# Output projection of a hybrid encoder block: high tokens against all four weight operands, then low tokens

## The chip, the cores and the metric

The kernel runs on one core of a Trainium2 chip. The metric is the device time of one execution in microseconds (us). The text speaks of the core's engines by their names in the profile: PE is TensorE's matmuls and PEld its weight loads, DVE is VectorE, ACT ScalarE, POOL GpSimd, SP the engine that issues most transfers.

## What is computed

One block over 2048 tokens and 16 meta tokens of width 1024, all in float32. Cut to what matters here:

```python
for layer in range(DEPTH):                                   # DEPTH = 1
    z = rms_norm(h, norm_gain[layer])
    proj = jnp.einsum("bld,de->ble", z, w_in[layer])
    q, k, v, g_attn, u_pool, g_pool = jnp.split(proj, SPLIT_POINTS, axis=-1)
    ...
    o_attn = chunked_window_attention(q, k, v, attn_sinks[layer])
    o_pool = multiscale_pool_mixer(u_pool, w_pool[layer], pool_scale[layer])
    gated = jnp.concatenate([jax.nn.silu(g_attn) * o_attn, jax.nn.silu(g_pool) * o_pool], axis=-1)
    h = h + jnp.einsum("ble,ed->bld", gated, w_out[layer])
return rms_norm(h, final_norm_gain)[:, N_META:]
```

The change is in the last product, `gated` (2048 tokens x 2048) times `w_out` (2048 x 1024).

## The kernel before, in words

**Splitting.** Every float32 operand of a large product is split into a high part (what the type fp32r keeps) and a low part (the rest). A product is then three matmuls: high times high, high times low and low times high. ScalarE makes the high part with a copy (L455 for weights, L651 for the tokens of the output projection), VectorE the low part with a subtraction (L694, L933).

**Stages.** The tokens are worked in two halves of 1024 (`h`). In each half come: the norm and the transposes of `x` (L1040); stage A, 18 blocks of input projection (function `project`, L1003 to L1005, weight blocks as stationary operand, 512 tokens as moving operand, all 24 matmuls of a call into one PSUM bank); stage B, 16 blocks of attention, each with scores (L1159 to L1161, four banks in turn), a projection block, transposes of the probabilities (L1185, L1187) and the product with the values (L1200 to L1203, one bank, `OB`); and stage C, the output projection (L1226 to L1228).

**Stage C.** It runs over two groups of 512 tokens (`tg`), and in each over 16 steps (`e`), one for each 128 rows of `w_out`: 64 steps in the whole kernel. A step holds four token tiles `t` of 128 tokens. For a tile the stationary operand is the tile's 128 x 128 block of gated tokens, high (`g_h`, from `gsh`) or low (`g_l`, from `gsl`), and the moving operand is 512 of the 1024 columns of the weight block, high (`w_h`) or low (`w_l`), for `dh` = 0 and 1. Tile `t` and column half `dh` have PSUM bank 2t + dh, so the eight banks hold the group's 512 x 1024 outputs and are summed over all 16 steps. A step is 24 matmuls. Weight blocks, their splits and the split tokens have two slots that alternate.

**What sets the order.** The instructions of each engine are written out by hand and held together by semaphores. For stage C:

- TensorE waits once at the head of a step for the low weights (`w_lo`) and the low tokens (`gs_lo`, or `gs_first` for the first step of a half). In the first step of a group it waits also ahead of some or all tiles, until the banks of that tile are free (`h_add`, `o_gate`, `pb_free`).
- The last matmul of a step signals `c_used`; ScalarE waits for it before it writes the high weights and high tokens of the step after next into the slot (L455, L651), VectorE follows (L694, L933), and SP may then load the next weight block into the raw slot (L264, waits for `w_lo`). GpSimd counts `c_used` too before it issues the loads of residual rows and of the next half's `x` (L428, L431).
- In the last step of a group the last matmul of each tile signals `c_done`. VectorE then adds the residual (L937), and the final norm and the store follow. In the very last group the last two steps are run for tiles 0 and 1, then 2, then 3.

The matmuls of a tile stand in the innermost loops of `step` (L1223 to L1228):

```python
for dh in range(2):
    w_h, w_l = wh[:, slot, dh * TB:dh * TB + TB], wl[:, slot, dh * TB:dh * TB + TB]
    co = ps[:, 2 * t + dh, :]
    te.matmul(co, g_h, w_h, start=first, stop=False)
    te.matmul(co, g_h, w_l, start=False, stop=False)
    last = te.matmul(co, g_l, w_h, start=False, stop=final)
```

Of the kernel before, what the change touches and what calls it, by code (L numbers as in the profile page):

```python
# [24 lines left out]
TB = 512  # L25
# [25 lines left out]
def build(nc, x, meta, wa, wu, wb, wp, wo, gain_n, gain_f, consts, ident_d, rot, rot_meta, out):  # L51
    wc = nc.dram_tensor("wc", (NG, 2, P, KT * P), F32, kind="Internal").ap()
    ctx = ExitStack()
    with ctx:
# [82 lines left out]
        wh, wl = wsplit[:, :, 0, :], wsplit[:, :, 1, :]  # L137
# [9 lines left out]
        ps = ctx.enter_context(nc.psum_tensor("ps", [P, 8, TB], F32))  # L147
# [55 lines left out]
        def block_c(h, tg, e):  # L203
            return BLOCKS * h + A_TILES + B_BLOCKS + C_STEPS * tg + e
# [769 lines left out]
        def _(pe):  # L974
            te = nc.tensor
# [93 lines left out]
            for h in range(HALVES):  # L1069
# [33 lines left out]
                if h == 0:  # L1103

                    pe.wait_ge(zm_step, 4)
                    for k in range(KT):
                        last = te.transpose(ps[:, SPARE, k * META:k * META + META], meta_rows[:, k * P:k * P + P], ident[0:META, 0:META])
# [22 lines left out]
                for m in range(NTT):  # L1130
                    last = te.transpose(ps[:, m // 4, (m % 4) * P:(m % 4) * P + P], wsum[:, m * P:m * P + P], ident[:, :])
# [17 lines left out]
                with pe.Fori(0, NG) as g:  # L1149
                    for sub in range(4):  # L1150
                        n = NCH * h + 4 * g + sub
                        slot = sub % 2

                        pe.wait_ge(qs_ready, n + 1)
                        for u in range(4):
# [5 lines left out]
                            last = te.matmul(so, q_l, k_h, start=False, stop=True)  # L1161
# [24 lines left out]
                        for u in range(4):  # L1186
                            last = te.transpose(ps[0:32, 2, u * P:u * P + P], probs[:, u, META0:KPITCH], ident[:, :])  # L1187
# [18 lines left out]
                for tg in range(TG):  # L1206
                    def step(e, slot, first=False, final=False, ts=range(TPG)):
                        pe.wait_ge(w_lo, block_c(h, tg, e) + 1)
                        if tg == 0 and first:
                            pe.wait_ge(gs_first, h + 1)  # L1210
                        else:
                            pe.wait_ge(gs_lo, (C_BLOCKS - 1) * h + C_STEPS * tg + e)
                        for t in ts:
                            if first and tg > 0:

                                pe.wait_ge(h_add, NTT * h + (tg - 1) * TPG + t + 1)
                            elif first and t == OB // 2:
                                pe.wait_ge(o_gate, NCH * (h + 1) + CREDIT)
                            elif first and t == PB[0] // 2:
                                for tb in range(NTB):  # L1220
                                    pe.wait_ge(pb_free[tb], FREES * (h + 1) + CREDIT)
                            g_h, g_l = gsh[:, slot, t * P:t * P + P], gsl[:, slot, t * P:t * P + P]
                            for dh in range(2):  # L1223
                                w_h, w_l = wh[:, slot, dh * TB:dh * TB + TB], wl[:, slot, dh * TB:dh * TB + TB]
                                co = ps[:, 2 * t + dh, :]
                                te.matmul(co, g_h, w_h, start=first, stop=False)  # L1226
                                te.matmul(co, g_h, w_l, start=False, stop=False)  # L1227
                                last = te.matmul(co, g_l, w_h, start=False, stop=final)  # L1228
                            if final:
                                last.then_inc(c_done, 1)  # L1230
                        if not final:
                            last.then_inc(c_used, 1)

                    step(0, 0, first=True)
                    step(1, 1)
                    with pe.Fori(1, C_STEPS // 2 - 1) as i:
                        step(2 * i, 0)
                        step(2 * i + 1, 1)
                    if h + 1 < HALVES or tg + 1 < TG:
                        step(C_STEPS - 2, 0)  # L1240
                        step(C_STEPS - 1, 1, final=True)
                    else:

                        for ts in ([0, 1], [2], [3]):
                            step(C_STEPS - 2, 0, ts=ts)
                            step(C_STEPS - 1, 1, final=True, ts=ts)
# [79 lines left out]
```

## Time and profile before

| | |
|---|---|
| median of 3 runs | 1353.28 us (1351.34 to 1355.07) |
| the profiled execution | 1353.39 us |
| its span, first to last instruction | 1351.7 us |
| mean granted TensorE clock | 0.994 |
| matmuls, and their busy time | 6293, 1318.0 us |
| of these in stage C | 1536 (L1226 to L1228) |

A busy time counts an engine's records with overlaps once. The records of consecutive matmuls overlap, since a matmul's record runs until its results are out and the next one has long started; so the distance from one start to the next is read from the timeline, not from the durations. Weight loads have records of their own (PEld) under the line of their matmul. An idle time with an arrow names what ended it.

### The profile page before, as it was taken

How to read it: one execution, taken by the hardware profiler on the slowest of the kernel's cores; microseconds unless marked ns; L12 is line 12 of the kernel's file. 1: busy time of each engine (PE TensorE's matmuls, PEld its weight loads, DVE VectorE, ACT ScalarE, POOL GpSimd, SP SyncE). 2: the span in 40 equal slices, each digit the busy share in tenths (PEclk: the TensorE clock that was granted, in tenths of full speed). 3: DMA queues.
4: the chain of work that ended last, by engine and by line, in shares of the span. 5: the costliest groups of instructions: out<-in, count | busy, mean ns of one | idle time of the engine just before them, and what ended most of it. 6: DMA issues, size and time to landing. Idle time of an engine off the chain costs nothing.

```text
span 1351.7 us, 18022 instructions
## 1 busy us (share of the span) xinstructions
PE 1318.0 (98%) x6293; PEld 1095.8 (81%) x6293; DVE 763.8 (57%) x1035; ACT 530.0 (39%) x1202; POOL 193.8 (14%) x260
## 2 busy tenths in 40 slices
PE   8899999999999999999999999999999999999997
PEld 8788888878787877888888888888878787788886
DVE  7443444476767675336456534447777767533635
ACT  6432222344444443225335222224444444322423
POOL 1121111211111111000001211121111111000000
PEclk8899999999999999999999999999999999999999
DMA  8511111110000004434442211110001010233442
GB/s 331 187 47 47 47 47 50 44 32 31 31 31 31 31 31 156 155 124 156 168 142 89 69 47 47 47 47 32 32 31 38 27 44 31 93 124 109 156 162 102
DMA packets 30397, 109.61 MB, mean 81 GB/s; under 512 B 3424, under 2 KB 3456, under 8 KB 30368
## 3 DMA queue, kind: packets, MB, share of 16 engines
q1 hardware_dynamic: 22032, 79.18, 17.0%
q0 software_dynamic: 8336, 30.05, 6.5%
q8 instruction: 17, 0.28, 0.1%
q14 instruction: 12, 0.10, 0.0%
HBM read 96.63 MB, written 12.58 MB: 81 GB/s over the span
## 4 chain that ended last, share of the span: by engine, by line
PE 58%; issue 28%; DVE 9%; DMA 2%; POOL 1%; ACT 1%; SPq 0%; DVEq 0%; POOLq 0%; ACTq 0%
PE ps L1227 9%; PE ps L1228 9%; PE ps L1226 9%; PE ps L1003 6%; PE ps L1004 6%; PE ps L1005 6%; DVE wsum L873 3%; PE ps L1185 2%; DVE stat L860 2%; DVE stat L863 1%; PE ps L1159 1%; PE ps L1161 1%; PE ps L1160 1%; PE ps L1187 1%; PE ps L1201 1%
## 5 line engine op out<-in xcount | busy, mean ns | idle before, releaser
L1003 PE MATMUL ps<-zh,wsplit 128*128 128x512 f32 x1072 | 422.4, 394 | 0.0
L1004 PE MATMUL ps<-zl,wsplit 128*128 128x512 f32 x1072 | 418.8, 391 | 0.0
L1005 PE MATMUL ps<-zh,wsplit 128*128 128x512 f32 x1072 | 418.1, 390 | 0.0
L694 DVE TENSOR_TENSOR wsplit<-wraw,wsplit 128x1024 fp32r<-128x1024 f32 x132 | 196.5, 1488 | 237.6 <-ACT wsplit L455 237.6
L1005 PEld LDWEIGHTS ps<-zh,wsplit 128*128 128x128 f32 x1072 | 201.4, 188 | 42.7
L1003 PEld LDWEIGHTS ps<-zh,wsplit 128*128 128x128 f32 x1072 | 201.5, 188 | 40.7 <-DVE wsplit L694 0.3
L1004 PEld LDWEIGHTS ps<-zl,wsplit 128*128 128x128 f32 x1072 | 201.5, 188 | 39.1
L455 ACT ACTIVATE wsplit<-wraw 128x1024 fp32r<-128x1024 f32 x132 | 139.7, 1058 | 227.2 <-PE ps L1228 217.3
L1228 PE MATMUL ps<-wsplit,gsl 128*128 128x512 f32 x512 | 203.3, 397 | 0.0
L1227 PE MATMUL ps<-wsplit,gsh 128*128 128x512 f32 x512 | 203.0, 396 | 0.0
L1226 PE MATMUL ps<-wsplit,gsh 128*128 128x512 f32 x512 | 199.7, 390 | 2.8 <-POOL gsl L413 2.5
L612 ACT ACTIVATE probs<-ps,stat 128x144 f32<-128x144 f32 x256 | 93.7, 388 | 133.8 <-DVE stat L863 133.8
L1226 PEld LDWEIGHTS ps<-wsplit,gsh 128*128 128x128 f32 x512 | 98.4, 192 | 26.3 <-issue 3.3
L1227 PEld LDWEIGHTS ps<-wsplit,gsh 128*128 128x128 f32 x512 | 96.2, 188 | 21.8
L1228 PEld LDWEIGHTS ps<-wsplit,gsl 128*128 128x128 f32 x512 | 96.2, 188 | 19.9
L355 POOL TENSOR_TENSOR rotsrc<-rotsrc,cos_t 128x1024 f32<-128x1024 f32 x18 | 61.6, 3420 | 324.5 <-DVE swapped L775 324.5
L595 ACT ACTIVATE wsum<-ps 128x512 f32<-128x512 f32 x64 | 38.5, 602 | 168.8 <-PE ps L1005 161.1
L795 DVE SCALAR_TENSOR_TENSOR gates_all<-wsum,ps 128x512 f32 x64 | 43.7, 682 | 73.3 <-ACT wsum L595 73.3
L396 POOL TENSOR_TENSOR kmask<-qk,cst 128x128 f32<-128x128 f32 x32 | 14.2, 443 | 385.6 <-PE ps L1161 385.1
L645 ACT ACTIVATE pth<-ps 128x512 fp32r<-128x512 f32 x64 | 34.8, 596 | 76.2 <-PE ps L1187 76.2
L539 ACT ACTIVATE rotsrc<-ps 128x512 f32<-128x512 f32 x32 | 19.1, 598 | 105.2 <-PE ps L1005 105.2
L775 DVE LOAD_MASK_SELECT swapped<-rotsrc x18 | 0.3, 14 | 104.8 <-issue 104.8
(160 smaller groups left out, 1575.2 us busy)
## 6 DMA issues: line engine op xcount, KB each, us to landing
wraw<-in_wo SPq DMA_DIRECT2D x64, 512.0 KB, 3.3
wraw<-in_wa SPq DMA_DIRECT2D x36, 512.0 KB, 3.3
wraw<-wc SPq DMA_DIRECT2D x16, 512.0 KB, 3.2
wraw<-in_wb SPq DMA_DIRECT2D x16, 512.0 KB, 3.2
rows<-in_x POOLq DMA_DIRECT2D x16, 512.0 KB, 4.3
xr<-in_x POOLq DMA_DIRECT2D x12, 512.0 KB, 5.6
curaw<-in_wu SPq DMA_DIRECT2D x8, 512.0 KB, 8.1
wc<-cout POOLq DMA_DIRECT2D x8, 512.0 KB, 4.5
```

Source lines behind the costliest of these rows:

```text
L355: gp.tensor_tensor(rotsrc[:, :], rotsrc[:, :], cos_t[:, :], ALU.mult).then_inc(rot_cos, 1)
L455: sc.activation(wh[:, slot, 0:size], wraw[:, slot, 0:size], ACT.Copy).then_inc(w_hi, 1)
L612: i = sc.activation(probs[:, u, kv * KEYS:kv * KEYS + KEYS], ps[:, u, kv * KEYS:kv * KEYS + KEYS], ACT.Exp, bias=negm[:, 2 * u + kv:2 * u ...
L694: ve.tensor_tensor(wl[:, slot, 0:size], wraw[:, slot, 0:size], wh[:, slot, 0:size].bitcast(F32), ALU.subtract).then_inc(w_lo, 1)
L795: ve.scalar_tensor_tensor(dst, wsum[:, tb * TB:tb * TB + TB], 1.0, ps[:, PB[tb], :], ALU.add, ALU.mult).then_inc(pb_free[tb], 1)
L873: ve.tensor_tensor_scan(wsum[:, :], ubuf[:, META:PRE + TOK], ubuf[:, bass.ds(META - (2 << g), META + TOK)], 0.0, ALU.add, ALU.subtract).th ...
L1003: te.matmul(ps[:, PB[bank], :], w_h, rhs_z(zh, tb, k), start=k == 0, stop=False)
L1004: te.matmul(ps[:, PB[bank], :], w_h, rhs_z(zl, tb, k), start=False, stop=False)
L1005: last = te.matmul(ps[:, PB[bank], :], w_l, rhs_z(zh, tb, k), start=False, stop=k == KT - 1)
L1226: te.matmul(co, g_h, w_h, start=first, stop=False)
L1227: te.matmul(co, g_h, w_l, start=False, stop=False)
L1228: last = te.matmul(co, g_l, w_h, start=False, stop=final)
```

## The change

For each token tile the two loops are taken apart. First the high tokens are multiplied with the high and low weights of both column halves, four matmuls, and then the low tokens with the high weights of both halves, two matmuls. The products, their number, their banks and the waits and signals around them stay as they are. Each bank's three products still come in the same order, with another bank's between them.

```diff
                             g_h, g_l = gsh[:, slot, t * P:t * P + P], gsl[:, slot, t * P:t * P + P]
+
                             for dh in range(2):
                                 w_h, w_l = wh[:, slot, dh * TB:dh * TB + TB], wl[:, slot, dh * TB:dh * TB + TB]
-                                co = ps[:, 2 * t + dh, :]
-                                te.matmul(co, g_h, w_h, start=first, stop=False)
-                                te.matmul(co, g_h, w_l, start=False, stop=False)
-                                last = te.matmul(co, g_l, w_h, start=False, stop=final)
+                                te.matmul(ps[:, 2 * t + dh, :], g_h, w_h, start=first, stop=False)
+                                te.matmul(ps[:, 2 * t + dh, :], g_h, w_l, start=False, stop=False)
+                            for dh in range(2):
+                                last = te.matmul(ps[:, 2 * t + dh, :], g_l, wh[:, slot, dh * TB:dh * TB + TB], start=False, stop=final)
                             if final:
                                 last.then_inc(c_done, 1)
```

## Rows read from the trace of the kernel before

**Rows 1.** The page: span, TensorE's busy time, granted clock in 40 slices.
```profile
span 1351.7 us, 18022 instructions
...
PE 1318.0 (98%) x6293; PEld 1095.8 (81%) x6293; DVE 763.8 (57%) x1035; ACT 530.0 (39%) x1202; POOL 193.8 (14%) x260
...
PEclk8899999999999999999999999999999999999999
```

**Rows 2.** TensorE's waits: us in total, times, longest.
```profile
PE ps L1226 <- POOL gsl L413: 2.5, 2, 1.2
```

**Rows 3.** Groups of the page: xcount, busy us, mean ns of one, idle before.
```profile
L1228 PE MATMUL ps<-wsplit,gsl 128*128 128x512 f32 x512 | 203.3, 397 | 0.0
L1227 PE MATMUL ps<-wsplit,gsh 128*128 128x512 f32 x512 | 203.0, 396 | 0.0
L1226 PE MATMUL ps<-wsplit,gsh 128*128 128x512 f32 x512 | 199.7, 390 | 2.8 <-POOL gsl L413 2.5
...
L1227 PEld LDWEIGHTS ps<-wsplit,gsh 128*128 128x128 f32 x512 | 96.2, 188 | 21.8
```

**Rows 4.** Stretch of stage C, first half: us, busy of PE, PEld, DVE, ACT, POOL.
```profile
522.70:700.20 177.50, 177.50 (x768) 145.41 (x769) 77.77 (x87) 61.99 (x88) 10.92 (x21) 1.00 0.46 157
```

**Rows 5.** Timeline in stage C: start us, us, engine, line; last row 24 matmuls later.
```profile
560.21 0.39 PE L1226 MATMUL ps<-wsplit,gsh 128*128 128x512 f32 x1
560.22 0.19 PEld L1227 LDWEIGHTS ps<-wsplit,gsh 128*128 128x128 f32 x1
560.44 0.40 PE L1227 MATMUL ps<-wsplit,gsh 128*128 128x512 f32 x1
...
565.76 0.39 PE L1226 MATMUL ps<-wsplit,gsh 128*128 128x512 f32 x1
```

**Rows 6.** Timeline of ScalarE and VectorE around one step of stage C.
```profile
556.34 1.06 ACT L455 ACTIVATE wsplit<-wraw 128x1024 fp32r<-128x1024 f32 x1 [3.97 <-PE ps L1228]
...
557.43 1.22 DVE L694 TENSOR_TENSOR wsplit<-wraw,wsplit 128x1024 fp32r<-128x1024 f32 x1 [3.72 <-ACT wsplit L455]
558.58 0.68 DVE L933 TENSOR_TENSOR gsl<-gates_all,gsh 128x512 fp32r<-128x512 f32 x1
...
561.89 1.06 ACT L455 ACTIVATE wsplit<-wraw 128x1024 fp32r<-128x1024 f32 x1 [3.97 <-PE ps L1228]
```

**Rows 7.** Transfers of the page: xcount, KB each, us from issue to landing.
```profile
wraw<-in_wo SPq DMA_DIRECT2D x64, 512.0 KB, 3.3
```

**Rows 8.** Timeline of TensorE in stage A; the second row is 96 matmuls later.
```profile
113.14 0.39 PE L1004 MATMUL ps<-zl,wsplit 128*128 128x512 f32 x1
...
134.90 0.39 PE L1004 MATMUL ps<-zl,wsplit 128*128 128x512 f32 x1
```

**Rows 9.** Timeline of TensorE, first step of stage C; the last is 6 later.
```profile
523.00 0.39 PE L1227 MATMUL ps<-wsplit,gsh 128*128 128x512 f32 x1
523.23 0.39 PE L1228 MATMUL ps<-wsplit,gsl 128*128 128x512 f32 x1
523.46 0.39 PE L1226 MATMUL ps<-wsplit,gsh 128*128 128x512 f32 x1
523.69 0.39 PE L1227 MATMUL ps<-wsplit,gsh 128*128 128x512 f32 x1
...
524.38 0.40 PE L1227 MATMUL ps<-wsplit,gsh 128*128 128x512 f32 x1
```

**Rows 10.** Timeline of TensorE, projection behind scores; 8 and 10 matmuls between the rows.
```profile
306.10 0.40 PE L1003 MATMUL ps<-zh,wsplit 128*128 128x512 f32 x1
...
307.95 0.39 PE L1005 MATMUL ps<-zh,wsplit 128*128 128x512 f32 x1
...
310.21 0.39 PE L1003 MATMUL ps<-zh,wsplit 128*128 128x512 f32 x1
```

**Rows 11.** Timeline of TensorE, product with the values; the second is 6 later.
```profile
268.45 0.39 PE L1200 MATMUL ps<-pth,vh 128*128 128x512 f32 x1
...
269.82 0.40 PE L1203 MATMUL ps<-ptm,vmeta 96*128 96x512 f32 x1
```

## The prediction, made before the change was run

> **What bounds the kernel now.** I read the head of the page first. TensorE's matmuls are busy for 98% of the span, and the granted clock is in its upper level, 2.4 GHz, in all slices but the first (0.8 there, and 9 stands for 90% or more) [rows 1]. The waits of TensorE come next: for its tokens the output projection waits 2.5 us in all, in two places, at its beginnings, out of a stage of hundreds of us [rows 2]. So this kernel ends when TensorE has issued its list. Only the number of its matmuls and the distance from one start to the next can move the end; a busy time can't, as the records overlap: one lasts 390 to 397 ns and the next starts after 0.23 us.
>
> **The stage that is changed.** L1226 to L1228 are 512 matmuls each, 1536 in all, and each has its own weight load [rows 3]. That holds for L1227 too, whose stationary block g_h is the one L1226 has just loaded: 512 loads of 188 ns that bring in what is already there. From 522.70 to 700.20, two token groups of one half, 768 matmuls take 177.50 us: 231.1 ns from start to start [rows 4]. Inside it, 24 starts take 565.76 - 560.21 = 5.55 us, again 231 ns; the load of L1227 begins 0.01 us after L1226 starts and takes 0.19, so it is over before its own matmul starts at 560.44 [rows 5]. Loads are hidden, and what counts is 1536 x 231.1 ns = 355 us of the 1351.7.
>
> **The change, step by step.**
>
> 1. Work: for one token tile 6 matmuls and 6 loads before, the same 6 and 6 after; per step 24 and 24. Nothing is added or taken away, so the plain sum is 0.
>
> 2. Waits: all stand ahead of the tile loop or of a tile, none inside the six, and each covers both banks of its tile. The second bank of a tile is first written by the third matmul of the six instead of the fourth, 0.23 us earlier, after the same wait: 0. The last matmul of a tile is the same one, low tokens into the second bank, so the signals c_done and c_used fire at the same place: 0 for the residual adds, for the final norm behind them, and for POOL's loads and stores that hang on c_used.
>
> 3. What is queued behind c_used: ScalarE's high weights start at 556.34, VectorE's low weights at 557.43 and low tokens at 558.58 for 0.68, ready at 559.26 [rows 6]. They are for the next step, which begins some 0.3 us ahead of ScalarE's next release at 561.89 [rows 6] (a matmul's record runs 0.17 us past the next start, and the signal is taken up after that); so about 2.3 us are spare. The weight transfer for a later step lands 3.3 us after its issue [rows 7], and it is issued when VectorE has split the block before, so it has over 2 us of the 5.55 us period left as well. Cost 0; the cover would be gone only if steps became over 2 us shorter, and 0.1 us is the most that is in question below.
>
> 4. The distances. This is the one unknown. The six transitions of a tile are now three kinds, each twice: same stationary, same bank (L1226 to L1227); new stationary, same bank (to L1228); new stationary, other bank (back to L1226). The modelled ends follow the next start at about 394.3 - 231.1 = 163 ns, so the group means 390, 396, 397 [rows 3] give 227, 233 and 234 ns for the three. After the change they are: same stationary and same bank twice; same stationary with other bank twice, which is new; new stationary with other bank twice. The new kind isn't in this stage's trace. It has a neighbour on each side, 227 and 234.
>
> For the whole stage I bound it by the rows around. The fastest long run of 512-column matmuls is the input projection: from 113.14 to 134.90 us 96 starts, 226.7 ns each [rows 8]. If the new order brought the stage there, it would gain 4.4 ns x 1536 = 6.8 us. If every transition became the slow one of today, 234 ns, it would lose 2.9 x 1536 = 4.5 us. Between them I take 231.1, no change, for two reasons. The first step of the stage shows the same transitions at one even distance: from 523.00 to 524.38 six transitions take 230 ns each in the mean, and the first three, a new stationary block, a change of bank and a repeated stationary block, read 0.23 us each [rows 9]. The split into 227, 233 and 234 comes only later, with the mean unmoved. And the input projection itself, with one bank and one pattern, runs 8 starts in 1.85 us, 231 ns, just after the score matmuls, and the next 10 in 2.26 us, 226 ns [rows 10]. So the extra 4 ns isn't the price of one kind of transition; it is a state the engine is in after other work, and in the output projection it stays.
>
> **Sum:** 0 against the profiled execution, 1353.39 us, whose span is 1351.7 with 1.7 around it. The median of the runs is 1353.28, 0.1 below; the forecast is 1353.3 us.
>
> **Rival 1, faster: a repeated stationary block is cheaper.** After the change four matmuls in a row hold g_h and two hold g_l, so four of six transitions repeat it where two did. Narrow form: each repeat costs 227, each renewal 233.5. A tile takes 4 x 227 + 2 x 233.5 = 1375 ns where it took 1388; 13 x 256 tiles (64 steps of four) = 3.3 us, giving 1350.0. Wide form: the longer runs settle the stage at the projection's 226.7, 6.8 us, giving 1346.5. For it: the 227 of L1227 in the settled stage. Against: the even first step [rows 9], and the input projection, where two of three matmuls renew the stationary block and all still start 226.7 ns apart [rows 8].
> The Trainium skill, "TensorE: Matmul & The Clock Gate", says in its step-by-step section that loads are separate so that one load can serve many matmuls, and under "Back-to-back issue gap" gives N/2.4 + 2.5 ns, 216 ns for 512 columns, for a matmul by itself. An estimate by that page, with 216 ns for the four repeats of a tile and 233.5 for the other two, is 1331 ns a tile, 57 x 256 = 14.6 us less than now. The trace doesn't bear that rule out: the repeats of today are loaded anew, and they take 227 ns.
>
> **Rival 2, slower: a change of PSUM bank costs.** The order changes bank 4 times per tile where it changed 2 times: 2 x 256 = 512 changes more. The price: the attention output product has the same high, high, low pattern into one bank and takes six starts in 269.82 - 268.45 = 1.37 us, 228.3 ns [rows 11]; the output projection with a change in every third takes 231.1, so a change would cost 2.8 x 3 = 8.4 ns. 512 x 8.4 = 4.3 us, giving 1357.6. It decides the sign from 4.06 us / 512 = 7.9 ns a change. For it: the transition that changes bank is the longest of the three. Against: in the first step it isn't [rows 9], and the 231 ns after the scores come without any change of bank [rows 10].
>
> **Rival 3: the change doesn't do what it says,** because equal loads would be dropped from the program. Now 512 of 512 are kept [rows 3], so I give it next to nothing.
>
> **How the numbers follow.** About 0.3% (4.06 us) is what a measurement of this kernel can tell from no change. No change 0.62; rival 1 0.21, of which 0.13 goes past 4.06 us; rival 2 0.14, of which 0.09 does; the rest 0.03 is split. Faster 0.14, same 0.76, slower 0.10. The predicted time is that of no change. The range goes from the wide form of rival 1, kept half a microsecond short because I doubt that the whole 6.8 comes, to just past rival 2 and the slow bound: 1347.0 to 1357.8.
>
> **What would show it.** Right: 1536 loads and 1536 matmuls still; the same 177.5 us for 768; ScalarE still released every 5.55 us; TensorE's waits unchanged. Rival 1: the stretch shortens by 1.6 to 3.4 us, and the matmuls that follow one with the same stationary block have the short records. Rival 2: the stretch grows by 2 us and the long records sit where the bank changes. Wrong altogether if the distance settles outside 227 to 234 ns, or if the third matmul of a tile has to wait for its bank.

## The result, and the profile after

The changed kernel took 1356.34 us (median of 20 runs, 1354.35 to 1358.33), the kernel before 1353.37 beside it (20 runs): ratio 1.0020, interval 1.0014 to 1.0026. The interval (95%) puts the loss at 1.9 to 3.5 us: small, inside the 0.3% that the prediction called no change, and inside its range, yet clear of zero. The profiled execution took 1355.79 us with a span of 1354.0, 2.3 more than before. The prediction said "no change" and had the work right, but the distances of step 4 do move, and neither rival says why. Two of its signs of being right aren't met: ScalarE is released every 5.58 us and not every 5.55, and the 768 matmuls of [rows 4] no longer fit into 177.50 us.

The page of the changed kernel: span and busy times, then the groups that answer to [rows 3] (the low tokens' matmul is now L1229).

```profile
span 1354.0 us, 18022 instructions
...
PE 1319.0 (97%) x6293; PEld 1091.9 (81%) x6293; DVE 763.9 (56%) x1035; ACT 531.0 (39%) x1202; POOL 194.1 (14%) x260
...
L1226 PE MATMUL ps<-wsplit,gsh 128*128 128x512 f32 x512 | 201.9, 394 | 2.8 <-POOL gsl L413 2.5
L1227 PE MATMUL ps<-wsplit,gsh 128*128 128x512 f32 x512 | 201.6, 394 | 0.0
L1229 PE MATMUL ps<-wsplit,gsl 128*128 128x512 f32 x512 | 161.3, 396 | 0.0
...
L1226 PEld LDWEIGHTS ps<-wsplit,gsh 128*128 128x128 f32 x512 | 96.1, 188 | 27.6 <-issue 3.3
```

The instructions are as many as before, 18022 in all, 6293 weight loads among them and 512 matmuls for each of the three lines, so equal loads are kept and rival 3 falls. The wait for the low tokens is the same 2.5 us. The granted clock isn't the cause either. In the stretch of [rows 4] it is 1.00 before, and the same stretch of the changed kernel has 1.00 too, with 762 matmuls where there were 768:

```profile
522.70:700.20 177.50, 177.24 (x762) 143.24 (x763) 76.76 (x86) 62.10 (x88) 11.23 (x22) 1.00 0.45 154
```

What differs is the record's mean: 390, 396 and 397 ns became 394, 394 and 396. The distance itself is read over many steps. ScalarE's L455 is released once per step, so its rows count steps; here it is first in the kernel before, then in the changed one, 27 steps between the two rows each time (start us, us, engine, line, and what ended the idle time).

```profile
534.15 1.06 ACT L455 ACTIVATE wsplit<-wraw 128x1024 fp32r<-128x1024 f32 x1 [4.05 <-PE ps L1228]
...
683.91 1.06 ACT L455 ACTIVATE wsplit<-wraw 128x1024 fp32r<-128x1024 f32 x1 [3.97 <-PE ps L1228]
```

```profile
534.48 1.06 ACT L455 ACTIVATE wsplit<-wraw 128x1024 fp32r<-128x1024 f32 x1 [4.08 <-PE ps L1229]
...
685.14 1.06 ACT L455 ACTIVATE wsplit<-wraw 128x1024 fp32r<-128x1024 f32 x1 [4.00 <-PE ps L1229]
```

Before, 27 steps in 149.76 us: 5.547 us each, and 24 matmuls a step are 231.1 ns apart. After, 27 steps in 150.66 us: 5.580 each, 232.5 ns apart. Over 1536 matmuls that is 1.4 x 1536 = 2.1 us, nearly all of the 2.3 by which the spans differ, and inside the 1.9 to 3.5 of the runs. So the loss is in the distances inside the stage, and not in a wait.

The timeline of one step shows where the distances sit. Starts of the first tile's matmuls and of a later tile's in the changed kernel ("x2" merges two rows):

```profile
560.70 0.40 PE L1226 MATMUL ps<-wsplit,gsh 128*128 128x512 f32 x1
560.94 0.40 PE L1227 MATMUL ps<-wsplit,gsh 128*128 128x512 f32 x1
561.17 0.39 PE L1226 MATMUL ps<-wsplit,gsh 128*128 128x512 f32 x1
561.40 0.40 PE L1227 MATMUL ps<-wsplit,gsh 128*128 128x512 f32 x1
561.63 0.62 PE L1229 MATMUL ps<-wsplit,gsl 128*128 128x512 f32 x2
...
563.49 0.39 PE L1226 MATMUL ps<-wsplit,gsh 128*128 128x512 f32 x1
563.72 0.39 PE L1227 MATMUL ps<-wsplit,gsh 128*128 128x512 f32 x1
563.95 0.39 PE L1226 MATMUL ps<-wsplit,gsh 128*128 128x512 f32 x1
564.17 0.40 PE L1227 MATMUL ps<-wsplit,gsh 128*128 128x512 f32 x1
564.41 0.64 PE L1229 MATMUL ps<-wsplit,gsl 128*128 128x512 f32 x2
564.89 0.40 PE L1226 MATMUL ps<-wsplit,gsh 128*128 128x512 f32 x1
```

The same line has different distances in different tiles: L1226 to L1227 takes 0.24 us at 560.70 and 0.22 at 563.95. The first is a tile's first pair and the second a tile's second pair, but both repeat the stationary block and keep the bank. Neither "a change of bank costs" nor "a repeat is cheap" can give that.

### The profile page after: what moved, and what is told of

Read it like the earlier page. It is cut to its first block, busy times and chain, and to the rows that moved or that the text cites. A ratio compares the mean times of both kernels' runs of the same rounds, so it can differ in the third digit from the quotient of the medians.

```text
span 1354.0 us, 18022 instructions
## 1 busy us (share of the span) xinstructions
PE 1319.0 (97%) x6293; PEld 1091.9 (81%) x6293; DVE 763.9 (56%) x1035; ACT 531.0 (39%) x1202; POOL 194.1 (14%) x260
## 4 chain that ended last, share of the span: by engine, by line
PE 59%; issue 28%; DVE 9%; DMA 2%; ACT 1%; POOL 1%; SPq 0%; DVEq 0%; POOLq 0%; ACTq 0%
PE ps L1229 9%; PE ps L1226 9%; PE ps L1227 9%; PE ps L1003 7%; PE ps L1004 6%; PE ps L1005 6%; DVE wsum L873 3%; PE ps L1185 2%; DVE stat L860 2%; DVE stat L863 1%; PE ps L1159 1%; PE ps L1161 1%; PE ps L1160 1%; PE ps L1187 1%; PE ps L1201 1%
## 5 line engine op out<-in xcount | busy, mean ns | idle before, releaser
L455 ACT ACTIVATE wsplit<-wraw 128x1024 fp32r<-128x1024 f32 x132 | 139.8, 1059 | 229.0 <-PE ps L1229 223.0
L1226 PE MATMUL ps<-wsplit,gsh 128*128 128x512 f32 x512 | 201.9, 394 | 2.8 <-POOL gsl L413 2.5
L1227 PE MATMUL ps<-wsplit,gsh 128*128 128x512 f32 x512 | 201.6, 394 | 0.0
L1229 PE MATMUL ps<-wsplit,gsl 128*128 128x512 f32 x512 | 161.3, 396 | 0.0
L1226 PEld LDWEIGHTS ps<-wsplit,gsh 128*128 128x128 f32 x512 | 96.1, 188 | 27.6 <-issue 3.3
L1229 PEld LDWEIGHTS ps<-wsplit,gsl 128*128 128x128 f32 x512 | 96.4, 188 | 22.2
L1227 PEld LDWEIGHTS ps<-wsplit,gsh 128*128 128x128 f32 x512 | 96.1, 188 | 22.5
```

The lines of the kernel that those rows point to most:

```text
L455: sc.activation(wh[:, slot, 0:size], wraw[:, slot, 0:size], ACT.Copy).then_inc(w_hi, 1)
L1226: te.matmul(ps[:, 2 * t + dh, :], g_h, w_h, start=first, stop=False)
L1227: te.matmul(ps[:, 2 * t + dh, :], g_h, w_l, start=False, stop=False)
L1229: last = te.matmul(ps[:, 2 * t + dh, :], g_l, wh[:, slot, dh * TB:dh * TB + TB], start=False, stop=final)
```

## The experiments

### The order of the products, in the whole kernel, and TensorE alone

Three other orders of the same six products, to separate the number of bank changes from the number of new stationary blocks; only the innermost lines of the step differ. `w_h` and `w_l` are here split in two halves.

```diff
 # banks_in_turn: 6 changes of bank a tile, stationary h h h h l l
-te.matmul(co, g_h, w_h, start=first, stop=False)      # per dh
-te.matmul(co, g_h, w_l, start=False, stop=False)
-last = te.matmul(co, g_l, w_h, start=False, stop=final)
+te.matmul(ps[:, 2 * t + 0, :], g_h, w_h[:, 0, :], start=first, stop=False)
+te.matmul(ps[:, 2 * t + 1, :], g_h, w_h[:, 1, :], start=first, stop=False)
+te.matmul(ps[:, 2 * t + 0, :], g_h, w_l[:, 0, :], start=False, stop=False)
+te.matmul(ps[:, 2 * t + 1, :], g_h, w_l[:, 1, :], start=False, stop=False)
+te.matmul(ps[:, 2 * t + 0, :], g_l, w_h[:, 0, :], start=False, stop=final)
+last = te.matmul(ps[:, 2 * t + 1, :], g_l, w_h[:, 1, :], start=False, stop=final)
 # snake: 3 changes, h h h h l l      high_low_high: 2 changes, h l h h l h
...
```

> Whole kernel; per tile the six products in the order high-high 0, high-high 1, high-low 0, high-low 1, low-high 0, low-high 1: the same runs of equal stationary blocks as in the changed kernel, but 6 changes of bank per tile where that has 4 and the kernel before 2. Bank theory: the changed kernel lost 2.1 us in this stage by 2 more changes a tile, so this one loses about 4.3 us against the kernel before (ratio 1.0032). Stationary theory: as the changed kernel, ratio 1.002. State theory: no order by the number of changes, anything between 0.995 and 1.003.

> Whole kernel; per bank the order high-high, low-high, high-low: banks change as in the kernel before (2 a tile), but the stationary block is a new one in 4 of 6 transitions, as before, now all with the bank kept, and the repeats fall on the bank changes. Bank theory: ratio 1.000. Stationary theory: a repeat at the bank change saves nothing on balance, 1.000 within 0.001. State theory: may differ by 0.001 to 0.002 either way.

> Whole kernel; per tile high-high 0, high-low 0, high-low 1, high-high 1, low-high 1, low-high 0: stationary runs as in the changed kernel, 3 changes of bank a tile instead of 4. Bank theory: 1 change more than the kernel before, +1.1 us, ratio 1.0008. Stationary theory: as the changed kernel, 1.002. State theory: not between the two.

Measured, against the kernel before: `banks_in_turn` 1.0018 (1.0009 to 1.0027), `high_low_high` 1.0001 (0.9992 to 1.0010), `snake` 1.0017 (1.0006 to 1.0028). In the traces, ScalarE's release rows of `banks_in_turn`, of `snake` and of `high_low_high`, 27 steps apart each:

```profile
534.15 1.06 ACT L455 ACTIVATE wsplit<-wraw 128x1024 fp32r<-128x1024 f32 x1 [4.09 <-PE ps L1229]
...
684.81 1.06 ACT L455 ACTIVATE wsplit<-wraw 128x1024 fp32r<-128x1024 f32 x1 [4.00 <-PE ps L1229]
```

```profile
533.20 1.06 ACT L455 ACTIVATE wsplit<-wraw 128x1024 fp32r<-128x1024 f32 x1 [4.09 <-PE ps L1229]
...
683.86 1.06 ACT L455 ACTIVATE wsplit<-wraw 128x1024 fp32r<-128x1024 f32 x1 [4.00 <-PE ps L1229]
```

```profile
535.46 1.06 ACT L455 ACTIVATE wsplit<-wraw 128x1024 fp32r<-128x1024 f32 x1 [4.05 <-PE ps L1229]
...
685.22 1.06 ACT L455 ACTIVATE wsplit<-wraw 128x1024 fp32r<-128x1024 f32 x1 [3.97 <-PE ps L1229]
```

150.66 us / 27 / 24 = 232.5 ns with six changes of bank a tile and the same 150.66 us with three (`snake`), exactly as in the changed kernel with four; 149.76 / 27 / 24 = 231.1 ns with two. The bank theory wanted 4.3 us more for six changes, 4.3 us / 1536 = 2.8 ns, so 233.9 ns; that isn't there. What the three slow orders share is the sequence of stationary blocks, four high and two low; what the old order and `high_low_high` share is a sequence that repeats every three. Among these five orders, with the buffers where they are, the distances follow the sequence of weight loads and not the banks. But more repeats come with the slower stage, so a repeat isn't cheap either.

Then TensorE alone, in a kernel that leaves out the block's computation and runs 14 loops of such matmuls, each of 240, over data in SBUF:

> TensorE alone: the block's computation is left out, and 14 loops of 240 matmuls of 128x512 run over data that lies in SBUF. Bank theory (each change of PSUM bank costs 4 to 8 ns): the old order reads about 231 ns from start to start, the new about 232.5, both fall to 226 to 227 when every output goes to one bank, two banks in turn reads 231 or more with all operands alike, and the input projection's pattern rises from 226.7 when it is given the changing banks. Stationary theory (a repeated stationary block is cheap, a new one dear): one bank changes nothing, a new stationary block each time is the slowest loop, all alike the fastest. State theory (neither): the distances of a loop depend on what ran before it, and the old and new order read differently when they come a second time.

Here are the new order (L76) and, with all operands alike, two banks in turn (L104), each from its first matmul to the first of the next loop:

```profile
82.06 0.39 PE L76 MATMUL ps<-wsplit,gsh 128*128 128x512 f32 x1
...
136.46 0.39 PE L83 MATMUL ps<-wsplit,gsh 128*128 128x512 f32 x1
...
299.66 0.39 PE L104 MATMUL ps<-wsplit,gsh 128*128 128x512 f32 x1
...
354.06 0.39 PE L111 MATMUL ps<-wsplit,gsh 128*128 128x512 f32 x1
```

54.40 us / 240 = 226.67 ns both times. All 14 loops read the same. Old order, new order, one bank, two banks in turn, all operands alike, a new stationary block or a new moving block each time, the input projection's pattern: after the first few matmuls of the first loop, each settled at 226.67 ns, and so did the repetitions. None of the three theories holds in this setting. The whole kernel's 231.1 and 232.5 needed something that wasn't there.

### What was missing: addresses, data, signals or a disturbance

> TensorE alone again, the block's computation left out: 12 loops of 240 matmuls, each behind 12 short matmuls of 288 columns as they stand in the attention, to disturb it. The first set of loops alone ran every order at 226.67 ns, so something of the kernel's setting is missing there. Address theory (weight load and moving read collide where the operands lie): with the operands at the kernel's own SBUF addresses the old order reads about 231.1 and the new about 232.5, at low addresses both 226.7. Data theory (split parts or full values matter): the loops with split data differ from those with full data. Signal theory (a wait and a signal at each step keep the disturbance alive): only the loops with waits and signals read 231 to 233. Disturbance theory: all loops begin at 231 to 235 behind the short matmuls and stay there. If all settle at 226.7 within some 10 matmuls, the cause is outside TensorE's own list: transfers or the other engines.

Each loop's distance is the time from its first matmul to the first of the short ones behind it, divided by 240:

| operands | old order | new order |
|---|---|---|
| low addresses | 226.7 | 226.9 |
| the kernel's addresses, both slots | 231.1 | 232.5 |
| the kernel's addresses, data split in high and low | 231.1 | 232.5 |
| the kernel's addresses, full data | 231.1 | 232.5 |
| the kernel's addresses, waits and signals per step | 231.1 | 232.5 |
| input projection's pattern, without and with waits | 226.7 | 226.9 |

(The last row has one pattern, without waits on the left. Where 226.9 stands beside 226.7, the first matmuls behind the short ones make the difference; both settle at 226.67.) The address theory is met to the tenth of a nanosecond. With TensorE alone, no transfers and the other engines idle, the kernel's two figures come back as soon as the operands lie where the kernel has them. Data, waits and signals make no difference. A disturbance by the short matmuls is there everywhere, single distances of up to 236 ns, but at low addresses and in the projection it is gone after three to ten matmuls.

### Which address

In the kernel the high tokens' buffer `gsh` begins at byte 209024 of a partition and the low tokens' `gsl` at 213248. That is 4096 bytes for the buffer and 128 more, because `gsl` shares the place of the tile behind `ubuf`, which is 32 elements longer than the tokens need. Modulo 256 (the remainder when the byte address is divided by 256) the weights and `gsh` lie at 128 and `gsl` at 0.

> TensorE alone, the block's computation left out: 24 loops of 144 matmuls, old and new order in turn, with the low tokens' buffer put at other bytes against the high tokens' buffer, and with the weights shifted. In the kernel the high tokens begin at byte 209024 of a partition, the low ones at 213248, 4096 + 128 bytes on. Offset theory (what counts is that the two stationary blocks lie differently against some block size of the memory): at the kernel's addresses 231.1 and 232.5; with the low tokens 128 bytes earlier, and at a distance of a whole 4096 bytes at low addresses, 226.7 for both; with +128 at low addresses 231.1 and 232.5 again; other distances differ. High address theory (the place above some address counts, not the offset): the 128 bytes change nothing at the kernel's addresses, and all loops at low addresses read 226.7. If the weights' own offset counts, the loops with both tokens or the weights shifted leave 226.7.

| operands | old order | new order |
|---|---|---|
| kernel's addresses | 231.1 | 232.5 |
| same, low tokens 128 B earlier | 226.8 | 227.0 |
| low addresses, low tokens +0 B | 227.0 | 227.0 |
| +32 B | 233.1 | 231.9 |
| +64 B | 231.1 | 231.2 |
| +128 B | 231.3 | 232.5 |
| +192 B | 231.1 | 230.6 |
| +256 B | 226.8 | 227.0 |
| +384 B | 231.1 | 232.5 |
| weights +0, both tokens +128 B | 232.3 | 233.3 |
| weights +128, both tokens +0 B | 233.3 | 232.4 |
| weights +128, both tokens +128 B | 226.9 | 227.0 |

The figures are means over 144 matmuls with the disturbed first ones among them. Here are the rows of the first four loops, old order (L84, L102) and new (L93, L111); the rows at L88, L97, L106 and L115 are the short matmuls behind each:

```profile
31.12 0.39 PE L84 MATMUL ps<-wk,gsh 128*128 128x512 f32 x1
...
64.40 0.29 PE L88 MATMUL ps<-wk,gsh 128*128 128x288 f32 x1
...
65.98 0.39 PE L93 MATMUL ps<-wk,gsh 128*128 128x512 f32 x1
...
99.45 0.29 PE L97 MATMUL ps<-wk,gsh 128*128 128x288 f32 x1
...
101.03 0.39 PE L102 MATMUL ps<-wk,gsh 128*128 128x512 f32 x1
...
133.68 0.29 PE L106 MATMUL ps<-wk,gsh 128*128 128x288 f32 x1
...
135.26 0.39 PE L111 MATMUL ps<-wk,gsh 128*128 128x512 f32 x1
...
167.95 0.42 PE L115 MATMUL ps<-w,g 128*128 128x288 f32 x2
```

144 matmuls take 33.28 us, 33.47, 32.65 and 32.69. Moving one buffer by 128 bytes removes the slow distance and, with it, the difference between the orders. Over the whole table, the distance is 226.8 to 227.0 ns (settled: 226.7) where the stationary blocks and the moving operand begin at the same byte modulo 256, and 230.6 to 233.3 everywhere else. Which order is the better one depends on the offset of the low tokens: the old by 1.2 to 1.4 ns at 128, the new by 1.2 at 32 and 0.5 at 192, neither at 64. The distance between the two operands modulo 256 isn't the whole rule. With both tokens 128 bytes off the weights, the old order is ahead by 1.0 when the tokens are the ones that moved, and the new by 0.9 when the weights are.

### The same in the whole kernel

```diff
-        gsl = at(wsum_at, "gsl", [P, 2, TB], F32R)
+        gsl = at(wsum_at - 128, "gsl", [P, 2, TB], F32R)
```

> The kernel before with one number changed: the low tokens' buffer of the output projection begins 128 bytes earlier, 4096 bytes behind the high tokens'. Offset theory: the stage's 1536 distances fall from 231.1 to 226.7 ns, 4.44 x 1536 = 6.8 us, so about 1346.6 us, ratio 0.995. High address theory: no change, 1.000.

> The changed kernel with the same number changed. Offset theory: 232.5 falls to 226.7 too, 5.83 x 1536 = 9.0 us less than the changed kernel, the same time as the aligned kernel before, ratio 0.995, and the order no longer matters. If the order has a cost of its own beside the offset, it stays 2 to 3 us above the aligned kernel before. High address theory: 1.002 as now.

Measured: the kernel before with this edit 0.9958 (0.9943 to 0.9972), the changed kernel with it 0.9949 (0.9936 to 0.9961). ScalarE's release rows, the aligned kernel before and then the aligned changed one, 27 steps apart each:

```profile
534.34 1.06 ACT L455 ACTIVATE wsplit<-wraw 128x1024 fp32r<-128x1024 f32 x1 [3.95 <-PE ps L1228]
...
681.22 1.06 ACT L455 ACTIVATE wsplit<-wraw 128x1024 fp32r<-128x1024 f32 x1 [3.75 <-PE ps L1228]
```

```profile
534.78 1.06 ACT L455 ACTIVATE wsplit<-wraw 128x1024 fp32r<-128x1024 f32 x1 [3.95 <-PE ps L1229]
...
681.66 1.06 ACT L455 ACTIVATE wsplit<-wraw 128x1024 fp32r<-128x1024 f32 x1 [3.86 <-PE ps L1229]
```

146.88 us for 27 steps in both: 226.7 ns. The spans are 1345.6 and 1345.5 us. So the order has no cost of its own: the 2.1 us appear only together with the offset.

The opposite test puts the buffer 32 bytes off instead of 128, where TensorE alone had the new order ahead:

```diff
-        gsl = at(wsum_at, "gsl", [P, 2, TB], F32R)
+        gsl = at(wsum_at - 96, "gsl", [P, 2, TB], F32R)
```

> The kernel before with the low tokens' buffer of the output projection 4096 + 32 bytes behind the high tokens' instead of 4096 + 128. Offset theory, by the loops with TensorE alone: the distance settles at 233.3 ns, 2.2 x 1536 = 3.4 us more than the kernel before, ratio 1.0025. If the order is what costs and the buffer's place is not, 1.000.

> The changed kernel with the same 32 bytes. Offset theory: 231.85 ns, 0.7 x 1536 = 1.1 us more than the kernel before, ratio 1.0008, so the same change of order now gains 2.3 us against the old order, where at 128 bytes it lost 2.1. If a change of bank or any cost of the new order itself were at work, it would lose 2 to 3 us here too.

Measured: old order 1.0020 (1.0011 to 1.0029), new order 1.0010 (1.0001 to 1.0019), against the kernel before. Against the kernel before the two intervals overlap. Against each other the eleven runs of each differ clearly: the medians are 1356.83 and 1354.25 us, nine of the old order's runs lie above 1355.3 and ten of the new order's below it. The rows say the same, old order first (27 steps), then new (26 steps):

```profile
536.15 1.06 ACT L455 ACTIVATE wsplit<-wraw 128x1024 fp32r<-128x1024 f32 x1 [4.11 <-PE ps L1228]
...
687.35 1.06 ACT L455 ACTIVATE wsplit<-wraw 128x1024 fp32r<-128x1024 f32 x1 [4.02 <-PE ps L1228]
```

```profile
540.37 1.06 ACT L455 ACTIVATE wsplit<-wraw 128x1024 fp32r<-128x1024 f32 x1 [3.06 <-PE ps L1229]
...
685.05 1.06 ACT L455 ACTIVATE wsplit<-wraw 128x1024 fp32r<-128x1024 f32 x1 [3.98 <-PE ps L1229]
```

151.20 / 27 / 24 = 233.3 ns for the old order, 144.68 / 26 / 24 = 231.9 for the new. The very change of this study, at another offset, shortens the stage by 1.4 x 1536 = 2.2 us. (In the second trace one weight transfer was late at 535.73; the count begins behind it.)

The groups of the old order at this offset also answer both rivals within one trace:

```profile
L1226 PE MATMUL ps<-wsplit,gsh 128*128 128x512 f32 x512 | 202.5, 395 | 2.8 <-POOL gsl L413 2.5
L1227 PE MATMUL ps<-wsplit,gsh 128*128 128x512 f32 x512 | 204.8, 400 | 0.0
L1228 PE MATMUL ps<-wsplit,gsl 128*128 128x512 f32 x512 | 199.2, 389 | 0.0
```

A longer record here means a later next start. At 128 bytes the shortest record was L1226's, 390 ns, behind which the stationary block is repeated, and the longest L1228's, 397, behind which the bank changes [rows 3]. At 32 bytes L1228's is the shortest, 389, and L1226's has 395: the repeat is no longer cheap, and the change of bank is no longer dear.

### Every operand of the large products aligned

```diff
-        arena = ctx.enter_context(nc.sbuf_tensor("arena", [P, (229344 - base - 64) // 4], F32))
+        arena = ctx.enter_context(nc.sbuf_tensor("arena", [P, (229344 - base) // 4], F32))
...
-        gsl = at(wsum_at, "gsl", [P, 2, TB], F32R)
+        gsl = at(wsum_at - 128, "gsl", [P, 2, TB], F32R)
...
-        cpl = at(wsum_at, "cpl", [P, 2, 2 * 2 * P], F32R)
+        cpl = at(wsum_at - 128, "cpl", [P, 2, 2 * 2 * P], F32R)
+        cursor[0] += 64
         vtok, vtok_at = place("vtok", [P, NTT, P])
```

> The kernel before, with every operand of a large product at the same byte modulo 256: the low tokens' buffer and the low part of the pooling map 128 bytes earlier, and all tiles behind them, the keys and values of the attention among them, 64 bytes later. Offset theory: the output projection at 226.7 ns as in the aligned kernel before; the product with the values falls from 228.3 to 226.7, and the projection behind the scores no longer runs its first matmuls at 231; together 1 to 3 us below the aligned kernel's ratio of 0.9958, so 0.993 to 0.995. If only the output projection is sensitive to it, 0.995 to 0.996.

Measured: 0.9952 (0.9939 to 0.9966), span 1343.7 us, a little above the 0.993 to 0.995 that was expected. Against the aligned kernel before, 0.9958, the intervals overlap, so the times don't separate them; the span is 1.9 us shorter in one profile each. One of the two effects that were expected is in the trace, the one on the product with the values, six starts from L1201 to L1204 (L1200 to L1203 one line further down):

```profile
269.06 0.39 PE L1201 MATMUL ps<-pth,vh 128*128 128x512 f32 x1
...
270.42 0.40 PE L1204 MATMUL ps<-ptm,vmeta 96*128 96x512 f32 x1
```

1.36 us / 6 = 226.7 ns, where [rows 11] gave 1.37 / 6 = 228.3. The values' tiles lay 64 bytes off the probabilities modulo 256 and now don't. Over 32 products of seven matmuls that is 1.6 x 7 x 32 = 0.4 us, so most of the 1.9 us isn't placed by it.

The other isn't there. The projection behind the scores was expected to lose its slow first matmuls; here it is, 8 and 9 matmuls between the rows:

```profile
306.62 0.40 PE L1004 MATMUL ps<-zh,wsplit 128*128 128x512 f32 x1
...
308.47 0.39 PE L1006 MATMUL ps<-zh,wsplit 128*128 128x512 f32 x1
...
310.51 0.39 PE L1006 MATMUL ps<-zh,wsplit 128*128 128x512 f32 x1
```

The first 8 still take 1.85 us, 231 ns each, as in [rows 10], and the next 9 take 2.04 us, 227 each. So the slow start behind short matmuls is there although the scores and the projection have all their operands aligned; alignment only decides that it fades.

## Why the prediction was right, and where its reasons failed

**What bounds the kernel, and steps 1 to 3: right.** The same instructions, the same waits, and ScalarE's splits and the transfers with time to spare. The whole difference is in the distance between starts, the one term that the prediction left open.

**Step 4: the wrong term.** It took 231.1 ns for every order, a cost of 0. Measured: 232.5, so + 1.4 x 1536 = 2.1 us. The figure lay inside the bounds of 226.7 and 234 that the rows gave, and this is why the range and "same" held. That the point of no change came so close is in part luck: no term knew the offset, which sets both the size and the sign of the difference. Both of its reasons were half right. "Not the price of one kind of transition" was shown: six, four and three changes of bank read alike, and so does everything when the operands are aligned. "A state the engine is in after other work" was the wrong half: slow distances do follow other work, as behind the scores [rows 10], but whether it fades (projection, within about ten matmuls) or stays (output projection) is set by where the operands lie. The lower bound, the projection's 226.7 [rows 8], was read as a bound that an order might reach; it is what an aligned stage does in any order.

**Rival 1 (a repeat is cheap): fell.** Four repeats a tile ran slower than two, and in the aligned setting repeat and renewal are both 226.7 ns. The 227 of L1227 before was one place in a pattern of three. The 216 ns that the Trainium skill, "TensorE: Matmul & The Clock Gate", gives under "Back-to-back issue gap" for a matmul of 512 columns by itself didn't appear: no matmul of 512 columns in any run here settled under 226.67 ns, not even with all operands the same for 240 in a row.

**Rival 2 (a change of bank costs): right in sign, wrong in cause.** Its price of 8.4 ns came from comparing the product with the values to the output projection. Those two differ in banks, but also in the offset of their operands, 64 bytes in one and 128 in the other, and the first is only seven matmuls long. Both fall to 226.7 once aligned, so neither distance holds a price of a bank; why the unaligned product reads 228.3 and not 231 isn't shown (64 bytes on the low tokens alone give 231.1). The price would have given 4.3 us; TensorE alone with two banks in turn gave 0.

**Rival 3: fell,** all 1536 loads are kept.

**What stays open:** how the memory makes the distance depend on the offset, and why a given sequence of loads settles at 231.1, 232.5 or 233.3. The runs show the map, not the mechanism. Also open is whether unaligned operands are slow by themselves: every unaligned loop stood behind short matmuls, as the stage in the kernel stands behind other work, and none was run undisturbed. And 2.1 of the 2.3 us between the spans are placed in the stage; the rest is as small as the spread of single executions.

## What to carry to other kernels

When matmuls stand back to back and still start a few ns further apart than in another stage with the same shapes, compare the byte offsets of the stationary and the moving operands before touching their order: here equal offsets modulo 256 bytes were worth 3.9 to 6.7 ns of 230.6 to 233.3, and in the kernel before, where it was 4.4 ns, that is 0.4% of its time for a one-number edit. A reordering that gains or loses a ns per matmul may be measuring that offset and will turn its sign when a buffer moves. And a stage can be taken out and run alone, but only with its addresses: the first such run, at convenient addresses, showed none of the effect.

## What the runs showed of the hardware that was not expected

- Back-to-back fp32r matmuls of 128x128 by 128x512, each with its own load, settle at 226.67 ns whatever the banks, the stationary blocks and the moving operands do, if all operands begin at the same byte modulo 256. With the low tokens, both tokens or the weights elsewhere they settle at 230.6 to 233.3 in the loops of this case, all of them behind short matmuls.
- The slow distance isn't even: in the changed kernel single distances run from 0.22 to 0.24 us and recur with the step. Three orders that share the sequence of loads and differ in banks and moving operands have the same mean, 232.5 ns.
- A short disturbance (12 matmuls of 288 columns) shows for three to ten matmuls in an aligned stream, and then it is gone.
